# Sign-split feed-forward kernel on one core: first norm taken from rows as they land, down-phase loads issued earlier at the hand-over, and the weight combinations of the unit loop placed behind the pair's

## The reference

```python
h = h + 0.5 * swiglu_ffn(rmsnorm(h, ffn1_norm), ffn1_w_in, ffn1_w_out)   # 1024 -> 2*2816 -> 1024
u = rmsnorm(h, mix_norm)
h = h + stick_breaking_attention(u, sb_w_qkv, sb_w_o, valid)             # 8 heads of 128
h = h + 0.5 * swiglu_ffn(rmsnorm(h, ffn2_norm), ffn2_w_in, ffn2_w_out)
out = rmsnorm(h, final_norm)                                             # meta tokens dropped
```

## Time and profile before

| | us |
|---|---|
| median of three runs | 1983.55 (1982.08 to 1986.01) |
| the profiled execution | 1982.76 |
| its span | 1981.0 |
| PE busy in the span | 1905.3 (96%) |
| DVE, POOL, ACT busy | 1318.2, 1089.1, 749.6 |

### The profile page before, as it was taken

How to read it: one execution, slowest core, us unless ns; L and a number is a source line. 1 busy time by engine, 2 the same in 40 slices (tenths; PEclk the granted TensorE clock), 3 DMA queues, 4 the chain that set the end, 5 groups by cost and what they waited for, 6 DMA issues and landing times. The chain is left out here.

```text
span 1981.0 us, 37412 instructions
## 1 busy us (share of the span) xinstructions
PE 1905.3 (96%) x12508; PEld 1739.0 (88%) x12508; DVE 1318.2 (67%) x1751; ACT 749.6 (38%) x1495; POOL 1089.1 (55%) x1010
## 2 busy tenths in 40 slices
PE   7899999999999999999999999999999999899997
PEld 6899999999999989999989987778877887778875
DVE  5877767676666768343389971297677767666676
ACT  5433343333222335222367762253334333322232
POOL 4456665655555645444477762355666566555560
PEclk9999999999999999999999999999999999999998
DMA  4234434355877411333232212014354435587732
GB/s 129 75 119 143 162 124 160 119 170 205 301 247 241 145 44 60 112 97 116 97 109 65 64 54 64 22 32 154 122 169 138 156 120 169 193 304 247 251 130 96
DMA packets 244612, 273.57 MB, mean 138 GB/s; under 512 B 12976, under 2 KB 176816, under 8 KB 244544
## 3 DMA queue, kind: packets, MB, share of 16 engines
q1 hardware_dynamic: 244544, 272.69, 41.8%
HBM read 179.58 MB, written 93.06 MB: 138 GB/s over the span
## 5 line engine op out<-in xcount | busy, mean ns | idle before, releaser
L1826 PE MATMUL psum<-arena 128*128 128x260 f32 (+3 forms) x3908 | 1245.7, 319 | 47.3 <-DVE scratch L1407 8.6
L1828 PE MATMUL psum<-arena 128*128 128x260 f32 (+3 forms) x3908 | 1228.6, 314 | 0.0
L1827 PE MATMUL psum<-arena 128*128 128x260 f32 (+3 forms) x3908 | 1226.2, 314 | 0.0
L1826 PEld LDWEIGHTS psum<-arena 128*128 128x128 f32 x3908 | 739.3, 189 | 106.6 <-issue 16.6
L1827 PEld LDWEIGHTS psum<-arena 128*128 128x128 f32 x3908 | 738.4, 189 | 45.5 <-issue 3.4
L1828 PEld LDWEIGHTS psum<-arena 128*128 128x128 f32 x3908 | 738.9, 189 | 43.6
L704 POOL TENSOR_TENSOR arena<-scratch,arena 128x512 fp32r<-128x512 f32 x365 | 516.4, 1440 | 409.8 <-ACT arena L952 409.8
L1407 DVE TENSOR_TENSOR scratch<-scratch,psum 128x520 f32<-128x520 f32 (+1 forms) x265 | 182.9, 690 | 247.4 <-PE psum L1828 188.1
L952 ACT ACTIVATE arena<-scratch 128x512 fp32r<-128x512 f32 x371 | 214.9, 622 | 319.1 <-DVE scratch L1410 117.2
L1410 DVE TENSOR_TENSOR scratch<-scratch 128x512 f32<-128x512 f32 x200 | 252.1, 1261 | 108.7 <-POOL arena L704 102.0
L796 POOL TENSOR_TENSOR arena<-scratch,arena 128x256 fp32r<-128x256 f32 x280 | 212.9, 780 | 180.7 <-ACT arena L1163 180.7
(11 more groups left out here) (93 smaller groups left out, 1296.1 us busy)
## 6 DMA issues: line engine op xcount, KB each, us to landing
scratch<-w_in_dram SPq DMA_DIRECT2D x88, 512.0 KB, 4.9
pairs<-scratch SPq DMA_DIRECT2D x140, 260.0 KB, 4.0
arena<-pairs SPq DMA_DIRECT2D x35, 1040.0 KB, 9.2
pairs<-scratch SPq DMA_DIRECT2D x140, 256.0 KB, 4.0
arena<-pairs SPq DMA_DIRECT2D x35, 1024.0 KB, 8.7
scratch<-w_out_dram SPq DMA_DIRECT2D x80, 256.0 KB, 3.1
qkv<-scratch SPq DMA_DIRECT2D x48, 260.0 KB, 2.1
scratch<-w_qkv_dram SPq DMA_DIRECT2D x24, 512.0 KB, 4.5
```

Of the source, the lines that this page charges most:

```text
L1826: nc.tensor.matmul(dst, wh, xh, start=start, stop=False, skip_group_check=True)
L1827: nc.tensor.matmul(dst, wh, xl, start=False, stop=False, skip_group_check=True)
L1828: return nc.tensor.matmul(dst, wl, xh, start=False, stop=stop, skip_group_check=True)
```

## The change

1. *First norm.* ACT squares the rows of x as they land, with a sum along the row (`square_x`), takes the root of nine columns and not of two banks; DVE takes the reciprocal of these; PE spreads them over the partitions by a matmul with the identity (`spread`). The plain weights are loaded before the last four tiles of x. DVE copies both halves of those tiles.
2. *Unit loop, FFN1 and FFN2.* `mix_last(u)` leaves the end of unit `u` and stands in unit `u+1`, behind the pair's operations and `y`. The store of B22's remainder moves from fifth to third of `store_second`. SP's order of loads and stores is otherwise the same in the loop.
3. *First units.* In unit 0 ACT splits the high parts of weights v0 and v6 before the last row part (v5), and not after it; in FFN1 two more splits and one row part move ahead of the silu.
4. *Hand-over.* The last unit's results go to free rooms (`last_rows`), so they wait for no store; the zeroed sums come last; SP issues the pair rows 0 and 1 first, then the first down weights, and further pair rows ahead of stores.

```diff
 def ffn_unit(u, second=False, pair=None, last=False):
+    up2, gate1, up1, gate2 = last_rows[n][0:4] if last else (c22, g0, u0, g1)
     if pair is not None:
         (first_tile if second else second_tile)(u, pair)
     product_over(u, 1)
     add(xy, xy, "b", "y")
+    if pair is not None:
+        mix_last(u - 1)
     ...
-    else:
-        dve.wait_ge(stored_second, 48 * pairs_to(pair + 1))
+    elif not last:
+        dve.wait_ge(stored_second, stored_to(n, pair + 1))
     ...
     if last:
         clear(sums_b[0], taken)
-    else:
-        mix_last(u)
     dve.wait_ge(s["silu1"], u + 1)
 ...
 def store_second(n, pair):
     store_part(n, "B21", pair, 0, x1, pair_hi, hi + 3, stored_second)
     store_part(n, "B22", pair, 0, x2, pair_hi, hi + 4, stored_second)
+    store_part(n, "B22", pair, 1, c22, pair_lo, lo + 3, stored_second)
     store_part(n, "T3", pair, 0, g1, pair_hi, hi + 5, stored_high)
     store_part(n, "T2", pair, 0, g0, pair_hi, hi + 6, stored_high)
-    store_part(n, "B22", pair, 1, c22, pair_lo, lo + 3, stored_second)
     store_part(n, "B21", pair, 1, u0, pair_lo, lo + 4, stored_high)
 ...
+def hand_over(n):
+    pairs_stored(n, pair)
+    room_free(n, 1)
+    load_pairs(n, 0, 0, (0, 1))
+    sp_eng.wait_ge(s["w_lo"], PRODUCTS * (UNITS[n] - 1) + 5)
+    sp_eng.wait_ge(s["mixed"], 4 * UNITS[n])
+    load_down_weights(n, 0, 0, 0, 0)
+    ...
 ...
 # ACT, unit 0
-    split_rows(n, 5)
-    first_out(0)
     act.wait_ge(s["w_loaded"], 64)
     weight_hi(n, 0)
     act.wait_ge(s["mixed"], 4)
     product_over(0, 3)
     weight_hi(n, 6)
+    split_rows(n, 5)
+    first_out(0)
 ...
 # start
+def square_x(t):
+    nc.scalar.activation(x_squares[0:n, t % 2], x_tiles[0:n, t], ACT.Square, accum_out=x_rstd[0:n, t:t + 1])
+def spread(c):
+    pe.wait_ge(rstd, c + 1)
+    ...
+for k, t in enumerate(X_TILES[1]):
+    take_low(t)
+    rows(FFN1, "B11", (k,))
```

More of the change, by code:

```diff
@@ L334, in sources_b @@
             return a11, s2_b, a21, s3_b, a12, a22, s4_b
+        last_rows = {n: [plain_regions[REGION_OF[n][v]][:, 2080 * late:2080 * late + HALF[n]]
+                         for v, late in ((3, 1), (4, 0), (4, 1), (5, 0), (6, 0))] for n in (FFN1, FFN2)}
         wd = {n: piece(region(REGION_OF[n][4]), 0, 2, 2, D_MODEL) for n in (FFN1, FFN2)}
@@ L482, in store_first, with store_second @@
                 store_part(n, "T1", pair, 1, x3, pair_lo, lo + 2, stored_first)
-            def store_second(n, pair, last=False):
+            def store_second(n, pair):
                 hi, lo = HI_ALL * (n // 2) + 7 * pair, LO_ALL * (n // 2) + 4 * pair
@@ L560, in ffn @@
                 store_first(n, HIDDEN_PAIRS - 1)
[L562 to L579, removed]
+                hand_over(n)
                 pairs_stored(n, HIDDEN_PAIRS)
@@ L1118, in ffn_unit @@
                         weight_hi(n, 0)
-                    if not second:
+                    if not second and not last:
                         last_difference_high(pair)
@@ L1123, in ffn_unit @@
                     weight_hi(n, 6)
-                    first_out(u, None if second else pair)
+                    first_out(u, None if second else pair, last)
                     if not last:
@@ L1328, in reciprocal, with rows @@
                 nc.vector.reciprocal(sums, sums).then_inc(rstd, 1)
-            def rows(n, name):
+            def rows(n, name, ks=range(HK)):
                 (kt, c), half = ROWS[name], HALF[n]
-                dve.wait_ge(rstd, 2 * n + c + 1)
-                for k in range(HK):
+                if n == FFN1:
+                    dve.wait_ge(summed, c + 1)
+                    dve.wait_ge(h_low, low_copies(X_TILES[c][-1]))
+                    dve.wait_ge(h_high, X_TILES[0][-1] + 1)
+                else:
+                    dve.wait_ge(rstd, 2 * n + c + 1)
+                for k in ks:
                     nc.vector.scalar_tensor_tensor(out=part(n, name, k),
@@ L1895, in plain_unit @@
                         last.then_inc(s["p_used"], 1)
+                        if n == FFN1 and i == 0:
+                            spread(1)
                 def first_unit():
@@ L2123, in _ @@
             pe.wait_ge(const_set, CONSTANTS)
-            for c in range(len(X_TILES)):
-                transpose_x(c)
-                sums(0, c)
+            for t in range(X_TILES[1][1]):
+                transpose_x(t)
+            spread(0)
+            for t in range(X_TILES[1][1], META_TILE + 1):
+                transpose_x(t)
             units(FFN1)
```

266 lines of the change are left out of this document (175 added, 91 removed).

## The result

The changed kernel takes **2147.78 us** (median of 4 runs, 2144.58 to 2148.44) against 1983.89 of the kernel before: a ratio of 1.0824, 95% interval 1.0809 to 1.0838. It is slower by 164 us; the forecast was 2100.6, with 2035 to 2155 as its range.

A forecast was written before the change was run, and what follows sets the result against it. PE, busy 96% of the span, was taken as the bound. Loops +62.1 and +60.3, first-tile units +9, start −11, hand-overs −7 and first units +4.4 made +117.8 on 1982.76: 2100.6 us, range 2035 to 2155.

The forecast's parts named there:

- The unit loops: Second-tile units: late mix_last delays loads and stores, PE stops before v5; +62.1 us in FFN1, +60.3 in FFN2.
- both contended: FFN1 second-tile unit: one second_tile operation and mix_last slowed by POOL, mix_last ending at 281.8; 281.0 was taken.
- The clock: Both unit loops: after each PE stop of over 2.5 us, a lower clock costs 1.6 us more.
- First-tile units of FFN2: mix_last behind y delays the gate load; 0.9 us in each of ten units, +9 (0 to 20).
- First units of QKV and FFN2: The same early splits without the new norm: 2.2 us each, +4.4 together (−3 to +6).
- The start: First norm and unit 0: normed rows and remainders begin sooner, less the cost of splits; −11 us together.
- its +2.2 for the splits: Unit 0: POOL's two weight remainders for v0 and v6 fall beside DVE's last row remainders, 1.1 us each.
- they hang on DVE alone: At the start: the remainders at 38.79 would begin at about 27.1, 11.7 us sooner, depending only on DVE.
- nothing collides: At the start: the favourable case, −14 us instead of −11.
- The hand-overs: Unit loop to down phase: clears wait less and pair rows load sooner; −7 us for both, between nothing and 12.
- Faster: Rival in the loops: the store still comes in time for v5, 1960.6 us; chance 0.10.
- A small stop: Rival in the loops: stores don't queue behind the two loads, stops of 1.9 us, +28, 2011 us; chance 0.07.

The follow-up runs named there:

- its parent: The changed kernel with mix_last(u) put back at the end of unit u on DVE, all other parts of the change kept: 1969.47 us, ratio 0.9936.
- the two troubles off: The changed kernel with mix_last and the late splits of v0 and v6 put back, plus one DVE wait for POOL in FFN1: 1956.68 us, ratio 0.9868.

## Why the prediction was right, and where it was short

- **The unit loops: right in mechanism, short by 23 us.** The queue was as told: gate load 0.2 after `mix_last`, third store 8.0 after the load (forecast 7.9), v5 0.87 after the landing (0.85). The term that was too small is when `mix_last` ends. I had 9.2 us from the silu's end (281.0 less 271.83), with 9.97 as the upper bound "both contended"; it was 9.97 (302.57 to 312.54). That both are 9.97 is partly luck: `second_tile` cost more than in the bound, since `hid1` and three of its operations took 1.6 to 1.8 each, and `mix_last` less, 1.21. The stops were 6.0 and 7.0 on average, and not 5.3 and 6.35 (5.1 over the present 1.25).
- **The clock: right sign, too small.** I took 1.6 us a stop, from the 2.50 us stop in the earlier trace rows. A turn of FFN1's loop became 8.1 us longer, 6.0 of stop and 2.1 on top. Over 18 stops the 0.5 makes 9 us.
- **First-tile units of FFN2: right.** Forecast 0.9 each, measured 1.0 on average by nine of them (0.6 to 1.8).
- **First units of QKV and FFN2: right.** Forecast +4.4; the stages took +2.8 and +2.0, and the run with the splits put back confirmed the cause: of the lead of 7.0 us that it has over its parent at unit 0 of FFN2, 3.4 come from FFN1 and 3.6 from these two.
- **The start: wrong, −1.4 for −11.** The gain itself was nearly there: the first product began at 24.92 for "near 24", DVE's remainders at 28.18 for 27.1, and with the two troubles off the start gained 10.3 us, where the forecast without its +2.2 for the splits has 13.2. The early splits cost 3.4 us in FFN1 (87.20 less 83.78), not 2.2. The step that failed is "they hang on DVE alone". PE also hung on POOL's remainder of row part v7, and POOL was held up by the very chain that I had moved forward, 5.1 us by `c12` (83.78 less 78.71). My "nothing collides" asked only whether POOL slows DVE, never the reverse.
- **The hand-overs: wrong, +8 for −7.** The run with `mix_last` put back gained 5.9 there, so the 7 was fair for the new order of loads by itself. In the changed kernel the down weights wait for the late `mix_last`, which I had named and yet allowed too little for. In FFN1's last unit SP issues two loads of pair rows, at 546.36 and 546.80, and the down weights only at 554.82, 0.1 after `mix_last`; with `mix_last` put back they follow the pair rows by 0.6 (473.69 and 474.27). What stands behind is late too: the last pair rows land 34.2 us after the first were issued, against 29.5. The two `clear` waits, 7.7 us before, still take 7.1. In FFN1 the waits of PE from unit 18 to QKV are 9.9 us against 5.4, which is the 4.5 of this stage. In FFN2 those of the hand-over are 8.2 against 9.2; what is worse there is the clock, 0.59 on average from 1895 to 1916, against 0.84 in the same 21 us of the kernel before (1728 to 1749). Which of the loads was short in each down phase stays open.
- **The rivals.** Faster was out, since the third store landed 8.0 us after the gate's issue and not within 2.6. A small stop, with stores that don't queue behind loads, was out by the same 8.0 against 4.5. In the turn shown the stores landed behind both loads and in the order of their issue. The Trainium skill, DMA: Bandwidth & Descriptors, section "Queues, rings and completion order", says that completion is not FIFO for one issuing engine. The whole trace agrees, by little: 20 transfers of SP's queue landed before the one issued just ahead of them, by 1.4 us at most. In FFN1's loop there was none, and in FFN2's three, by 0.3 at most, so it made nothing faster here.

The misses have the signs +9.6 (start), +10.2 and +12.6 (loops), +15 (hand-overs) and +0.4: all to the slow side, 48 us together. Each time I had allowed too little for engines and a queue that now meet; that this holds for other changes is not shown.

## What to carry to other kernels

Before an instruction is moved for the sake of its own engine, ask what it frees: here its last read of a buffer let a load go, the load stood ahead of stores in one queue, and the stores freed a buffer that DVE had to have for `w`, without which PE could not begin v5, 11 us after the read (273.37 to 284.66). Follow a move through every queue that waits on its semaphore, with the landing time of the first transfer and of all that stand behind it. And a part that is split "sooner" is only free if the engine that works on it is not then working beside the one that everything waits for.

## What the runs showed of the hardware that was not expected

- **POOL can be shut out for many instructions.** DVE in the changed kernel, at the start:

```profile
38.99 2.52 DVE L1461 TENSOR_TENSOR arena<-plain,arena 128x520 fp32r<-128x520 f32 x4
41.43 2.52 DVE L1451 TENSOR_TENSOR scratch<-plain,scratch 128x520 f32<-128x520 f32 x4
43.87 1.90 DVE L1451 TENSOR_TENSOR plain<-plain 128x520 f32<-128x520 f32 x3
47.02 1.68 DVE L1451 TENSOR_TENSOR plain<-plain 128x520 f32<-128x520 f32 x1 [1.25 <-POOL arena L780]
```

  DVE ran eleven operations between SBUF tiles (the expectation says twelve) at 0.61 us from start to start (4.88 us for eight, between the first and the third row), from 38.99 to 45.77. The POOL operation started at 38.98 lasted all that time and 1.15 us more, 7.94 in all, and then DVE itself had to wait for it. With DVE held back until POOL was done, it took 1.3. The Trainium skill, SBUF — State Buffer, section "SBUF: two separate sides", says that the port pair is an exclusive lock, held by one instruction, and the other "fully blocks". The trace agrees that POOL was blocked, and goes further: it stayed blocked over eleven DVE instructions, as if the next one got the pair again each time. Elsewhere both went on side by side, with 1.6 to 1.8 us for DVE's operations and some 1.7 for POOL's. What decides between the two patterns I have not shown.
- **Beyond its length, a stop of PE cost much the same, whether it was 4 or 8 us long.** By the length of FFN1's turns, the clock and small waits took 2.2 us after stops of 4.0 (the stores ahead of the load), 2.1 after 6.0 (the changed kernel) and 2.3 after 7.6 (`mix_last` alone moved). After 2.5 us idle it was 1.6, by the matmuls of the earlier trace rows.
